# Cross-attention of a two-block network: queries computed turned, pairs ordered by heads then tiles

## The reference, cut to what matters

```python
def second_block(...):
    for l in range(DEPTH):                       # DEPTH = 2
        ...                                      # even or odd self-attention, added to x
        h = rms_norm_2(x, g[2])
        y = memory_cross_attention(h, mem, xa_wq[l], xa_wkv[l], xa_wo[l], xa_mem_norm[l])
        x = x + rms_norm_2(y, g[3])
        h = rms_norm_2(x, g[4])
        ...                                      # squared-ReLU MLP, added to x
```

## Time and profile before

| what | value |
|---|---|
| median of 3 runs | 1367.0 us (1366.8 to 1367.0) |
| the profiled execution's own time | 1366.88 us |
| its span, first to last instruction | 1365.1 us |
| PE busy | 1353.9 us, 99% |
| DVE busy | 1007.8 us, 74% |
| ACT busy | 744.8 us, 55% |
| POOL busy | 110.8 us, 8% |
| chain that ended last | PE 97%, DVE 1%, ACT 1% |

### The profile page before, as it was taken

The page is one execution under the profiler, slowest core; times in us unless marked ns, Lnnn a source line. Parts: engine busy times, 40 slices in busy tenths (PEclk is TensorE's granted clock), DMA queues, the critical chain, the costliest instruction groups (busy, mean ns, idle before and its releaser), DMA issues.

```text
span 1365.1 us, 19457 instructions
## 1 busy us (share of the span) xinstructions
PE 1353.9 (99%) x7455; PEld 1132.5 (83%) x7455; DVE 1007.8 (74%) x1518; ACT 744.8 (55%) x1155; POOL 110.8 (8%) x112
## 2 busy tenths in 40 slices
PE   9999999999999999999999999999999999999998
PEld 6887888888888888888888778888888878888886
DVE  5566878777764767977788777887667887786665
ACT  4564655555455654555554666654445675654443
POOL 0000011000000000211111001220000001400000
PEclk9999999999999999999999999999999999999999
DMA  9844456555565335666655523458875424366562
GB/s 314 238 152 154 147 181 197 185 186 186 184 211 181 133 124 160 223 203 204 205 193 174 165 93 124 139 199 213 219 214 188 161 102 155 124 202 196 188 188 90
DMA packets 146579, 242.26 MB, mean 177 GB/s; under 512 B 4604, under 2 KB 91404, under 8 KB 146223
## 3 DMA queue, kind: packets, MB, share of 16 engines
q1 hardware_dynamic: 142498, 226.97, 51.2%
q0 software_dynamic: 3712, 13.77, 3.7%
q10 hardware_dynamic: 276, 0.27, 0.1%
HBM read 239.03 MB, written 1.97 MB: 177 GB/s over the span
## 4 chain that ended last, share of the span: by engine, by line
PE 97%; DVE 1%; ACT 1%; issue 0%; POOL 0%; DVEq 0%; ACTq 0%
PE ps L1132 19%; PE ps L1096 17%; PE ps L1105 16%; PE ps L1102 16%; PE ps L1137 10%; PE ps L1242 3%; PE ps L1305 2%; PE ps L1320 2%; PE ps L1351 1%; PE ps L1923 1%; PE ps L1181 1%; PE ps L1178 1%; PE ps L1184 1%; PE ps L1933 1%; PE ps L1500 1%; PE ps L1502 1%
## 5 line engine op out<-in xcount | busy, mean ns | idle before, releaser
L2584 DVE TENSOR_TENSOR wlo<-raw,whi 128x1024 fp32r<-128x1024 f32 (+2 forms) x423 | 528.4, 1260 | 189.0 <-ACT whi L2045 187.7
L2045 ACT CAST whi<-raw 128x1024 fp32r<-128x1024 f32 (+1 forms) x431 | 444.7, 1042 | 262.6 <-PE ps L1105 161.7
L1132 PE MATMUL ps<-act,whi 128*128 128x512 f32 x1152 | 315.3, 394 | 0.0
L1096 PE MATMUL ps<-whi,mhi 128*128 128x512 f32 (+2 forms) x688 | 236.3, 392 | 0.7 <-issue 0.7
L1105 PE MATMUL ps<-whi,mlo 128*128 128x512 f32 (+2 forms) x688 | 231.4, 385 | 0.0
L1102 PE MATMUL ps<-wlo,mhi 128*128 128x512 f32 (+2 forms) x688 | 231.2, 385 | 0.0
L1132 PEld LDWEIGHTS ps<-act,whi 128*128 128x128 f32 x1152 | 199.4, 189 | 28.4
L1137 PEld LDWEIGHTS ps<-act,wlo 128*128 128x128 f32 x1152 | 177.7, 189 | 24.9
L1137 PE MATMUL ps<-act,wlo 128*128 128x256 f32 x1152 | 184.2, 281 | 0.0
L1102 PEld LDWEIGHTS ps<-wlo,mhi 128*128 128x128 f32 x688 | 129.2, 188 | 26.6 <-DVE wlo L2584 0.5
L1105 PEld LDWEIGHTS ps<-whi,mlo 128*128 128x128 f32 x688 | 129.2, 188 | 26.6
(11 more groups left out here) (328 smaller groups left out, 1547.3 us busy)
## 6 DMA issues: line engine op xcount, KB each, us to landing
raw<-in_mlp_w SPq DMA_DIRECT2D x64, 1024.0 KB, 5.3
raw<-in_w_up SPq DMA_DIRECT2D x44, 1024.0 KB, 5.2
raw<-in_w_in SPq DMA_DIRECT2D x38, 1024.0 KB, 5.1
raw<-in_w_down SPq DMA_DIRECT2D x22, 1024.0 KB, 5.1
raw<-in_ev_w_in SPq DMA_DIRECT2D x10, 1024.0 KB, 5.1
raw<-in_w_out SPq DMA_DIRECT2D x8, 1024.0 KB, 5.2
raw<-in_xa_wkv SPq DMA_DIRECT2D x4, 1024.0 KB, 5.5
raw<-in_ev_w_out SPq DMA_DIRECT2D x4, 1024.0 KB, 5.2
```

Of the source, the lines that this page charges most:

```text
L1096: nc.tensor.matmul(o, hi[:, kx, rows_], wh[:, k, c0:c0 + w], start=first and h == 0 and k == 0 and (tt == 0 or at[1] == 0), stop=False)
L1132: nc.tensor.matmul(both, wh[:, k, w], act2[:, kx].rearrange("p i n -> p (i n)"), start=kx == 0, stop=False)
L2045: nc.scalar.copy(whi[:, m % HL, 0:w], raw[:, n % RAW, h * w:h * w + w]).then_inc(hi_done, 1)
L2584: nc.vector.tensor_tensor(wlo[:, m % HL, 0:w], raw[:, n % RAW, h * w:h * w + w], whi[:, m % HL, 0:w].bitcast(F32), ALU.subtract).then_inc( ...
```

## The change

The query product swaps its sides: slices of wq of 128 columns are stationary and all 256 tokens move, so that q comes out with the heads on the partitions, block b (heads 2b and 2b+1) in bank 6 + b. The turns of q, the copies to `proj` and the copies of the turned result go; ACT copies each bank straight to `qT` times SCALE, without the norm's factor. That factor is given to the exponential as its scale, one number for each token, where there was the constant -1. The scores are no longer negated, so `lows` takes a maximum and then multiplies it, in a second small DVE instruction that waits for the first, by the factor and by -1. The pairs are ordered heads 0 and 1 of tile 0, heads 0 and 1 of tile 1, heads 2 and 3 of tile 0, heads 2 and 3 of tile 1, and PE computes `scores(0)` before the last quarter of the query product. On DVE all four `lows` now stand ahead of the first copy, and the copies' order is pairs 0, 2, 1; on PE the turns of pairs 1 and 2 come ahead of the first values. The last wait that is left ahead of `cross_out(0, 0)` is for the high parts; the low parts are waited for after its first four matmuls.

```diff
@@ -229,8 +229,6 @@
             plan.group(("xx", l, g), "split")
         plan.job(("wq", l), [(KD, 256, [(0, 256, rows(a["xa_wq_2"][l], 0, KD, 0, 256))])])
         plan.group(("qkx", l, 0), "dve")
-        plan.group(("qkx", l, 1), "act")
-        plan.group(("qkx", l, 2), "dve")
         for tt in range(TT):
             plan.group(("ox", l, tt), "dve")
         plan.job(("wo", l), tall(a["xa_wo_2"][l], 0, 2))
...
@@ -580,7 +577,8 @@
                 heads = odd_heads()
             us = [head_unit(qt, *h) for j in range(0, len(heads), 2) for qt in range(TT) for h in heads[j:j + 2]]
             stages.append((("even" if l % 2 == 0 else "odd", l), us))
-            stages.append((("cross", l), [head_unit(qt, *h) for qt in range(TT) for h in cross_heads()]))
+            heads = cross_heads()
+            stages.append((("cross", l), [head_unit(qt, *h) for j in range(0, HX, 2) for qt in range(TT) for h in heads[j:j + 2]]))
         first_unit, n_units = {}, 0
         units_of = {}
         for k, us in stages:
@@ -604,7 +602,7 @@
                 else:
                     eng = (("dve", "dve", "dve", "act") if d["deep"] else ("act", "dve", "dve", "dve"))[i // 2 % 4]
                 n_copies[eng] += d["wide"] or i % 2 == 0
-                copied_by.append((eng, n_copies[eng]))
+                copied_by.append((eng, n_copies[eng] + ((0, 1, -1, 0)[i // 2] if d["deep"] else 0)))
 
         n_joint = 2 * HB * TT // 2
@@ -771,8 +769,6 @@
 
             if key[0] == "qk2" and key[2] in (2, 3):
                 return 2
-            if key[0] == "qkx" and key[2] == 2:
-                return 5
             if key[0] == "ox":
                 return 2 + key[2]
             if key[0] == "y1" and key[2] == "b":
@@ -1844,45 +1840,45 @@
                 sxx["turn_to"](0)
                 memory_half(l, "k", 1, 2, middle=lambda: sxx["turn_to"](3))
 
-                def query(tt, gs):
-
-                    n = plan.jobs["wq", l][0]
-                    for g in gs:
-                        m = 2 * n + g // 2
-                        if tt == 0:
-                            if g % 2 == 0:
-                                wait_lo(pe, m)
-                            sxx["need"](g)
-                        wh, wl = (w[:, m % HL, :].rearrange("p (k n) -> p k n", k=KD // 2) for w in (whi, wlo))
-                        o = ps[:, 6 + tt, 0:SEQ]
-                        rows_ = slice(tt * P, tt * P + P)
-                        for k in (2 * g, 2 * g + 1):
-                            nc.tensor.matmul(o, mhi[:, k, rows_], wh[:, k % 4, :], start=k == 0, stop=False)
-                            m0 = nc.tensor.matmul(o, mhi[:, k, rows_], wl[:, k % 4, :], start=False, stop=False)
-                            m1 = nc.tensor.matmul(o, mlo[:, k, rows_], wh[:, k % 4, :], start=False, stop=k == KD - 1)
-                        if tt == 0:
-                            sxx["turn_to"](g + 2)
-                            if g == 3:
-                                m1.then_inc(q_out, 1)
-                        elif g % 2:
-                            m0.then_inc(pe_out, 1)
-                            m1.then_inc(pe_out, 1)
-
-                def turn_query(tt):
-
-                    pe.wait_ge((q0_ready, q1_ready)[tt], l + 1)
-                    turn_blocks(("qkx", l, 1 + tt), [proj[:, tt, b * P:(b + 1) * P] for b in range(2)])
+                def query(b, g):
+
+                    m = 2 * plan.jobs["wq", l][0] + g // 2
+                    if b == 0:
+                        if g % 2 == 0:
+                            wait_lo(pe, m)
+                        sxx["need"](g)
+                    wh, wl = (w[:, m % HL, :].rearrange("p (k n) -> p k n", k=KD // 2)[:, :, b * P:b * P + P] for w in (whi, wlo))
+                    o = ps[:, 6 + b, 0:SEQ]
+                    for k in (2 * g, 2 * g + 1):
+                        nc.tensor.matmul(o, wh[:, k % 4, :], mhi[:, k, 0:SEQ], start=k == 0, stop=False)
+                        m0 = nc.tensor.matmul(o, wl[:, k % 4, :], mhi[:, k, 0:SEQ], start=False, stop=False)
+                        m1 = nc.tensor.matmul(o, wh[:, k % 4, :], mlo[:, k, 0:SEQ], start=False, stop=k == KD - 1)
+                    if b == 0 and g == 3:
+                        m1.then_inc(q_out, 1)
+                    if b == 1 and g % 2:
+                        m0.then_inc(pe_out, 1)
+                        m1.then_inc(pe_out, 1)
 
                 def cross_out(tt, c):
 
                     n = plan.jobs["wo", l][0]
                     o = ps[:, yxb(tt, c), :]
+                    rows_ = slice(tt * P, tt * P + P)
+                    if tt == c == 0:
+                        pe.wait_ge(cross_high, TT * l + 1)
+                        for h in range(2):
+                            wait_lo(pe, 2 * n + h)
+                            for t, w in enumerate((whi, wlo)):
+                                nc.tensor.matmul(o, mhi[:, h, rows_], w[:, (2 * n + h) % HL, 512 * c:512 * c + 512], start=h == t == 0, stop=False)
+                        pe.wait_ge(cross_low, TT * l + 1)
+                        for h in range(2):
+                            m1 = nc.tensor.matmul(o, mlo[:, h, rows_], whi[:, (2 * n + h) % HL, 512 * c:512 * c + 512], start=False, stop=h == 1)
+                        m1.then_inc(wo_out, 1)
+                        return
                     for h in range(2):
                         m = 2 * n + h
-                        if tt == c == 0:
-                            wait_lo(pe, m)
                         wh, wl = (w[:, m % HL, 512 * c:512 * c + 512] for w in (whi, wlo))
-                        xh, xl = (t[:, h, tt * P:tt * P + P] for t in (mhi, mlo))
+                        xh, xl = (t[:, h, rows_] for t in (mhi, mlo))
                         nc.tensor.matmul(o, xh, wh, start=h == 0, stop=False)
                         m0 = nc.tensor.matmul(o, xh, wl, start=False, stop=False)
                         m1 = nc.tensor.matmul(o, xl, wh, start=False, stop=h == 1)
@@ -1958,37 +1954,37 @@
                     for g in range(4):
                         low_weights(1, g)
 
-                query(0, range(4))
+                for g in range(2):
+                    for b in range(2):
+                        query(b, g)
                 pe.wait_ge(ev_act, evs_act2(l, "k"))
                 turn_blocks(("qkx", l, 0), [kvn[:, tt, b * P:(b + 1) * P] for b in range(2) for tt in range(TT)])
-                query(1, (0, 1))
-                turn_query(0)
-                query(1, (2, 3))
-                pe.wait_ge(grp_dve, plan.by_number[plan.groups["qkx", l, 0]][2])
-                pe.wait_ge(grp_act, plan.by_number[plan.groups["qkx", l, 1]][1])
+                query(0, 2)
+                query(0, 3)
+                query(1, 2)
                 scores, turn, values = attention_steps(("cross", l))
 
                 def both_of(step, p):
                     step(2 * p)
 
+                pe.wait_ge(grp_dve, plan.by_number[plan.groups["qkx", l, 0]][2])
+                pe.wait_ge(q_ready, 2 * l + 1)
                 scores(0)
+                query(1, 3)
                 scores(2)
-                turn_query(1)
-                pe.wait_ge(grp_dve, plan.by_number[plan.groups["qkx", l, 2]][2])
+                pe.wait_ge(q_ready, 2 * l + 2)
                 scores(4)
                 both_of(turn, 0)
                 scores(6)
                 both_of(turn, 1)
-                pe.wait_ge(at_e, first_unit["cross", l] + 5)
+                both_of(turn, 2)
                 both_of(values, 0)
-                both_of(turn, 2)
+                both_of(turn, 3)
                 turn_shares(0)
+                both_of(values, 2)
                 both_of(values, 1)
-                both_of(turn, 3)
-                both_of(values, 2)
+                both_of(values, 3)
                 turn_shares(1)
-                both_of(values, 3)
-                pe.wait_ge(cross_low, TT * l + 1)
                 cross_out(0, 0)
                 cross_out(0, 1)
                 pe.wait_ge(cross_low, TT * l + 2)
@@ -2456,14 +2452,12 @@
                 memory_product(l, "k", 2)
                 split_half(n0 + 13)
 
+                act.wait_ge(q_out, l + 1)
+                nc.scalar.activation(qT[:, 0, 0:SEQ], ps[:, 6, 0:SEQ], ACT.Copy, scale=SCALE).then_inc(q_ready, 1)
+                split_half(n0 + 14)
+                wait_turned(act, plan.jobs["wq", l][0])
+                nc.scalar.activation(qT[:, 1, 0:SEQ], ps[:, 7, 0:SEQ], ACT.Copy, scale=SCALE).then_inc(q_ready, 1)
                 act.wait_ge(rstd_ready, rs_count["xx", l])
-                act.wait_ge(q_out, l + 1)
-                nc.scalar.activation(proj[:, 0, 0:256], ps[:, 6, 0:256], ACT.Copy, scale=rstd[:, NORM["xx", l], 0:1]).then_inc(q0_ready, 1)
-                key = ("qkx", l, 1)
-                group_ready(act, key)
-                nc.scalar.activation(qT[:, 0:2, 0:P], ps[:, bank_of(key), 0:SEQ].rearrange("p (b n) -> p b n", b=2), ACT.Copy,
```

(39 more changed lines are left out.)

## The result

The changed kernel takes 1372.54 us (median of 6 runs, 1372.01 to 1373.64) against 1366.9 us before (1366.31 to 1367.06). The ratio is 1.0043, with a 95% interval from 1.0031 to 1.0054: slower by 5.6 us, or 0.4%. Forecast were 1370.3 us, in a range that ended at 1372.0.

What follows compares the result with a forecast made beforehand. PE, busy 1353.9 of 1365.1 us, was taken as the bound. Per layer -0.42 in front, +1.10 and +0.86 for two waits and 0.12 at pair 1's turn gave +1.66, +3.3 in all: 1370.3 us, range 1367.8 to 1372.0.

Steps and rivals of the forecast that it cites:

- The query product: PE's 48 query matmuls of 256 columns: swapping sides costs nothing, 0.281 us each against 0.28.
- The exponentials: ACT's eight exponentials: scale from memory adds 0.09 us each, 0.56 apart; first pair turn still 0.42 us a layer sooner.
- Behind the first turn: PE after pair 0's turn: waits for DVE's copies, 1.10 us at the turn of pair 2, 0.86 at pair 3.
- The output product: Start of the output matmuls: waiting for high parts costs nothing; later low-parts wait gains at most 0.06 us.
- The maxima: DVE's reduction plus small instruction: 0.93 us to the value, was 0.69; 0.85 to the next instruction, was 0.61.
- the clock: Rival: PE's two waits bring the grant to 1.2 GHz, 24 output matmuls slower, +5.5 us a layer, 1381; chance 0.03.
- Durations used: Step and hand-over times read from the earlier profile, such as 0.59 us for a pair's turn or values step.
- the first rival: PE's last seven steps run faster after a stall, 0.1 us each, -0.7 a layer, 1368.9 us; chance 0.22.

Runs made afterwards that it cites:

- the first experiment: Changed kernel, but DVE copies pair 0 ahead of the maxima of pair 3 and pair 1 ahead of pair 2: 1368.78 us, ratio 1.0014.
- order, no factor: Changed kernel with DVE's copies back in PE's order and the norm's factor left out of the cross-attention: 1365.10 us, ratio 0.9985 against the kernel before.
- no factor: Changed kernel with the norm's factor left out of the cross-attention (constant exponential scale, maxima in one instruction): 1369.54 us, ratio 1.0017 against the kernel before.

## Why the prediction was wrong

**Right, as the prediction put it.** "The query product": nothing is lost by swapping the sides. From the turn of k to the end of the first 36 matmuls it is 1.88 us in both kernels, and the first scores step starts 2.69 us behind the turn of k (1163.39, 1166.08), as forecast (866.01, 868.70). "The exponentials": 0.56 us each. "Behind the first turn": waits of 1.10 and 0.86 us were forecast at the turns of pairs 2 and 3, 0.87 and 0.89 were measured in layer 1, and the first experiment shows that the order on DVE causes them. So the direction and its main reason were right. "The output product": no gain, shown in the kernel before alone.

**Two steps failed: the term of "The maxima", and the clock, which was put at next to nothing.** At full clock the changed kernel would have stayed in the range: with the waits filled it took 1371.06. What carried the time beyond 1372.0 is the clock in layer 0. By the account below, too, two layers at full clock come to 1366.9 + 4.5 = 1371.4 us, inside the range.

**"The maxima"** took 0.93 us from the start of a reduction to the value for each pair. Measured in layer 1 were 1.41 (1166.92 to 1168.33) and 2.25 (1168.39 to 1170.64) for pairs 0 and 1, and 1.02 for pairs 2 and 3. The term left out that POOL runs two weight splits through the front of the stage. That put the turn of pair 2 at 9.85 us behind the turn of k where 8.88 was forecast (874.89 less 866.01); with the maxima in PSUM it was at 8.81. The Trainium skill states the mechanism (SBUF — State Buffer, "SBUF: two separate sides"): VectorE and GpSimd share a pair of ports to SBUF, and an instruction that needs it waits until the other engine's has finished. The trace agrees, with two ends 0.02 us behind POOL's, and with 0.22 us once the maxima are in PSUM; which ports the small instruction used no trace here shows. The trace of the kernel before already had a case. Of the two instructions behind the earlier trace rows one took 0.17 us, and the prediction took that one; this is the other:

```profile
825.85 0.49 DVE L3300 TENSOR_SCALAR small<-small 128x4 f32<-128x4 f32 x1
```

It ends at 826.34, and an instruction of POOL that had begun at 825.28 ends at 826.32. In the cross-attention before, POOL's two splits run from 868.56 to 873.25, across the place where the change puts its small instructions.

**The clock** was given a chance of 0.03 and a price of 5.5 us a layer, for 24 output matmuls at half pace. The argument against it was that no row showed a fall around a stand of 0.52 us; that was one stand, where the changed kernel had already stood 0.26 and 0.65 us when the grant fell in its third, of 0.86. The place was wrong too: the fall lay on turns and values, from 874.3 to 881.1, and was over before the first output matmul at 881.56. It cost 2.21 us in one layer.

**A reading that doesn't hold.** "Durations used" has the turn of a pair start 0.61 us behind the start of the pair's second exponential (871.67, 872.28). There PE came straight from a scores step, so the row shows PE's queue and no hand-over. After the change the turn of pair 0 starts 0.16 behind it (1168.97, 1169.13), since its first unit needs the first exponential alone, and then its step takes 0.91 us where 0.59 was forecast (1169.13 to 1170.04), since the second unit waits inside it. The two errors partly cancel: the scores step behind it begins 6.65 us behind the turn of k (1163.39, 1170.04) where 6.44 was forecast.

**A term that was too large.** From the start of the turn of pair 3 to the output product 2.93 us were forecast, and 2.47 were measured (1175.34 to 1177.81): three values steps behind each other take 1.47, 0.49 each, where they took 0.59 with turns between them. That is the size of the first rival, but not its reason: without any stall, in "order, no factor", the same stretch takes 2.49 (1168.17 to 1170.66), so what counts is that the values steps stand together. It was luck for the forecast, as it offsets 0.46 of what the maxima cost.

**The account.** A layer at full clock was forecast at +1.66. The turn of pair 2 comes 0.97 later than forecast (1.04 from the stand behind POOL, less 0.07 elsewhere), the turn of pair 3 another 0.06, and the shorter tail takes 0.46: +2.23, the measured value. Layer 0 adds 2.21 for the clock. Both stages together make 4.44 + 2.23 = 6.67 us. The profiled executions differ by 5.13 (1372.01 and 1366.88), since the changed one reached the stage of layer 0 1.08 us earlier and spent 0.44 less between the stages. The first lies ahead of everything that the change touches, and the stage of layer 0 begins up to 3.6 us apart in these executions; the second isn't explained. The medians differ by 5.6 us, not by 6.67 less 0.44, or 6.2; the rest isn't placed either, as only one execution was profiled.

**Still open.** Why the clock fell in layer 0 and not in layer 1 of the changed kernel, whose waits are alike (0.26, 0.65, 0.86 us, and 0.26, 0.65, 0.87), isn't settled. With PSUM and unfilled waits of 1.05 and 0.89 us it fell in both, and in "no factor" with 0.99 and 0.89 in neither. That filling the waits keeps the clock up is shown; which stands bring it down isn't.

## What to carry to other kernels

When an instruction is moved on an engine's queue, write down who waits for what is now behind it: the copies that free a bank stand in a cycle with the turns that fill it, and one line in the wrong place cost 1.05 us here, whatever else the change gained. A factor moved from one pass over the data into many small steps has to be priced at each of them; here it took back 0.83 of 0.96 us, and bringing it in once, as a row, kept 0.70 of the 0.96. PE's stands have a price beyond their length, as the clock may fall in them: here 2.21 us in one layer. Before adding a small VectorE instruction that reads and writes SBUF, look at what GpSimd runs at that time.

## What the runs showed of the hardware

- A TENSOR_SCALAR of 128x2 in SBUF took 0.61 and 1.45 us while POOL was in a 128x1024 TENSOR_TENSOR, until that ended, 0.23 us otherwise, and 0.22 with the maxima in PSUM while POOL ran the same splits. The reductions and copies out of PSUM in the same stretch kept their 0.68 to 0.69.
- The granted clock fell to 1.2 GHz in layer 0 of the changed kernel inside a stand of 0.86 us, behind stands of 0.26 and 0.65 us among short steps. In layer 1, with the same stands, it didn't. Eight unneeded matmuls in the two longer waits kept it at 2.4 GHz in both, and cost at most 0.05 us (14.42 and 14.47 in the stages, against 14.42).
- A second operand from memory makes an ACTIVATE of 128x256 0.09 us longer (0.47, 0.56). The Trainium skill (ScalarE: Activation LUTs, "What ACT_TABLE_LOAD costs") gives the same price for each such operand; the trace agrees.
- A DVE instruction that waits for the one ahead of it started 0.79 to 0.80 us behind the start of a 128x512 reduction (1166.92, 1167.72), an unlinked one 0.61.
